# Two-block transformer on one core: in the attention of layers 0 and 1, TensorE multiplies by the values and turns the values ahead of the next step's scores instead of behind them

## The chip, the cores and the metric

One core of a Trainium2 chip runs the whole program. The metric is the device time of one launch in microseconds (us), the median over several runs.

## What is computed

Two blocks of two transformer layers each, in float32, on 512 latent tokens and 256 context tokens of width 1024. Layers 0 and 1 (the first block) hold the attention that the change touches: four heads, and in each head two softmax maps over the same keys, of which the second is subtracted with a weight:

```
def diff_attn(q, k, v, lam):
    s = jnp.einsum("bqhmd,bkhmd->bhmqk", q.astype(F32), k.astype(F32)) * (B_QK_DIM ** -0.5)
    p = jax.nn.softmax(s, axis=-1)
    a = p[:, :, 0] - lam * p[:, :, 1]
    return jnp.einsum("bhqk,bkhd->bqhd", a, v.astype(F32))
```

The latent queries attend to all 768 tokens. In layer 0 the 256 context queries attend to the 256 context tokens as well; in layer 1 the context has no queries. Around the attention stand the input projection, a gated part, a convolution, the output projection and a feed-forward part, and the second block has other kinds of attention; none of that changes.

## The kernel before

Every engine has its own list of instructions, written out in Python and executed in order; the engines meet through semaphores. Weights pass through a ring of slots, are split into a high and a low part, and TensorE forms each linear layer as three products. Nearly every matmul is issued by the helper `mm`, line 1161, so that line names scores, products with values and linear layers alike; they are told apart by their operands.

**Steps and rounds.** `Attention.__init__` (from line 721) cuts the attention into steps: for each head four blocks of 128 latent queries, and in layer 0 a fifth step with both blocks of context queries (keys: 256). That makes 20 steps in layer 0 and 16 in layer 1. TensorE's `attention` (the loop `for n in range(A.n)` from line 1645) runs in rounds. Round n holds, for step n-3, the turns of the finished map (`turn`, line 1552: six 128x128 transposes through PSUM, in two groups of three, p0 and p1; for a context step one group of four), then the scores of step n+1 (`scores`), and behind them what else the planner put in this round (`rr[2:]`): either the product of the turned maps with the values (`values`, operands `PTR` and `VT`) of the pair of blocks that ends at step n-4, or the turns of a later head's values (line 1558, a group of four, v0, and one of two, v1). Products come in every second latent round. In a round whose map is a context step there is only one group of map turns, so the product is the second entry and already stands ahead of the scores.

Where the planner's list `rr` is made (lines 766 to 788), each entry gets a number r, counted through the layer. Turns and products all write the bank `AUX`:

```
        def turn_bank(r):

            return AUX[:, 512 * (r["n"] % 2):512 * (r["n"] % 2) + 512]
```

Its two halves alternate by number, and `bank_free` makes entry r wait until entry r-2 has been read out.

**The other engines.** VectorE's `attention` finds the maxima of step n+1 for both maps (line 2875, the `TENSOR_REDUCE`), inverts the sums of the exponentials and subtracts the maps (line 2912). GpSimd scales the first map (line 1056). ScalarE's `attention` runs, in round n, in this order: the exponentials of step n's first map (`exps(n, 0)`, line 2143), the copy of the product of round n-1 out of the bank (line 2129), the copies of this round's map turns into `PTR` (line 2118), the exponentials of the second map, and at the end the copies of turned values (line 2122).

**Score buffers.** The scores of the two maps take three PSUM buffers in turn, `PS[(2 * n + e) % 3]`, so `scores(n + 1)` waits for `exps(n, 0)` before it overwrites the buffer.

`keep_clock` in round 2 issues seven idle-time matmuls; it keeps its place.

Of the kernel before, what the change touches and what calls it, by code (L numbers as in the profile page):

```python
# [109 lines left out]
def build(nc, d, out):  # L110
# [81 lines left out]
    with ctx:  # L192
# [266 lines left out]
        for li, L in enumerate(layers):  # L459
# [18 lines left out]
            for part, rr in enumerate((rows, second)):  # L478
                r, todo = 0, []
# [58 lines left out]
        def stat_use(li, name):  # L538

            return len(STAT_USES) * li + STAT_USES.index(name)  # L540
# [613 lines left out]
        def _(pe):  # L1154
# [15 lines left out]
            def keep_clock(n, bank):  # L1170

                for _ in range(n):
                    mm(bank[:, 0:P], IDENT, IDENT, True, True)

            def tile(t, kc, toks, hi, lo, out=None, mid=None, chunk=None, spare=False, ctx_ready=None):

                slot = t % 2
                pe.wait_ge(S.hi_ready, t + 1)
                if t >= 2 and not spare:
                    pe.wait_ge(S.tile_free, t if out is not None else t - 1)  # L1180
                out = AUX if spare else LIN[slot] if out is None else out
                for a, n in spans(toks):
                    if a and ctx_ready:
                        ctx_ready()
                    for k in range(kc):
                        if chunk and a == 0:
                            chunk(k)
                        mm(out[:, a:a + n], whi(t)[:, k, :], hi[:, k, a:a + n], k == 0, False)
                        mm(out[:, a:a + n], whi(t)[:, k, :], lo[:, k, a:a + n], False, False)
                if mid:  # L1190
                    mid()
                pe.wait_ge(S.lo_ready, t + 1)
                for a, n in spans(toks):
                    for k in range(kc):
                        last = mm(out[:, a:a + n], wlo(t)[:, k, :], hi[:, k, a:a + n], False, k == kc - 1)
                last.then_inc(S.tile_done, 1)
# [57 lines left out]
            def piece(t, i):  # L1254

                if i == 0:
                    pe.wait_ge(S.hi_ready, t + 1)
                if i == 2:
                    pe.wait_ge(S.lo_ready, t + 1)
                for a, n, high, ks in (((0, LAT, True, range(0, 5)),), ((0, LAT, True, range(5, 8)), (LAT, CTX, True, range(0, 4))),  # L1260
                                       ((LAT, CTX, True, range(4, 8)), (LAT, CTX, False, range(8))), ((0, LAT, False, range(8)),))[i]:
                    for k in ks:
                        if high:
                            mm(AUX[:, a:a + n], whi(t)[:, k, :], HH[:, k, a:a + n], k == 0, False)
                            mm(AUX[:, a:a + n], whi(t)[:, k, :], HL[:, k, a:a + n], False, False)
                        else:
                            last = mm(AUX[:, a:a + n], wlo(t)[:, k, :], HH[:, k, a:a + n], False, k == DC - 1)
                if i == 3:
                    last.then_inc(S.tile_done, 1)
# [254 lines left out]
            def attention(A, L):  # L1524
# [105 lines left out]
                def step(r):  # L1630

                    (values if r["kind"] == "o" else turn)(r)
# [12 lines left out]
                for n in range(A.n):  # L1645
                    rr = A.rounds[n]
                    if n == 0 and A.diff:
                        pe.wait_ge(S.stat_read, stat_use(li, "turn V0") + 1)
                    for i in A.pieces.get(n, ()):
                        piece(A.late.t0, i)  # L1650
                    if n and n - 1 == A.evac_at:
                        pe.wait_ge(S.tile_free, A.late.t0 + 1)
                    for r in rr[:2]:
                        step(r)
                    if n in A.tiles:
                        x = A.tiles[n]
                        hi, lo = (CQH, CQL) if x.kc == 6 else (CKH, CKL)
                        tile(x.t0, x.kc, x.toks[0], hi, lo, STAT)
                    if A.mla:
                        for r in rr[2:]:  # L1660
                            step(r)
                    if n < 3:
                        keep_clock(((13, 0, 0) if A.mla else (0, 0, 7) if A.diff else (0, 8, 0))[n], STAT if A.mla else AUX)
                    if n + 1 < len(A.steps):
                        for part in range(2):
                            scores(n + 1, part)
                    if not A.mla:
                        for r in rr[2:]:
                            step(r)
                pe.wait_ge(S.exp_done, A.sides_end())  # L1670
# [19 lines left out]
            for li, L in enumerate(layers):  # L1690
# [86 lines left out]
                if blk == 0:  # L1777
                    pe.wait_ge(S.norm_used, norm_at(li, "Q3") + 1)
                    pe.wait_ge(S.mod_copied, 1)
                    pe.wait_ge(S.half_read, half_use(li, "w_s") + 1)  # L1780
                    attention(L["attention"], L)
                    rs_read()
                    head_sums, head_spread = norm_parts(T, False, big)
# [9 lines left out]
                elif l == 0:  # L1793
                    pe.wait_ge(S.qk_ready, w.seen(S.qk_ready))
                    pe.wait_ge(S.swap_landed, 32)
                    attention(L["attention"], L)
                else:
                    key_sums, key_spread = norm_parts(TOK, False, lambda c: RCK[:, c, :])
                    query_sums, query_spread = norm_parts(LAT, False, lambda c: RCQ[:, c, :])
                    n0 = w.made.get(S.rs_done, 0)  # L1800
                    def latent_jobs(j):
                        if j == 3:
                            rs_read()
                            key_sums(n0, (0, 1))
                        if j == 4:
                            key_spread(n0)
                    linear(L["w_in"], HH, HL, None, S.h_ready, mid=latent_jobs, pause=9)
                    q0, k0, v0 = L["heads"][0]
                    pe.wait_ge(S.cq_ready, w.seen(S.cq_ready, 2))
                    linear(k0, CKH, CKL)  # L1810
                    query_sums(n0 + 1, range(6))
                    linear(v0, CKH, CKL)
                    query_spread(n0 + 1)
                    keep_clock(14, AUX)
                    w.seen(S.mix_hi, 4 * 2 + 2)
                    linear(L["q_rope"], CQH, CQL, None, S.cq_ready, range(6))
                    linear(q0, CQH, CQL)
                    rs_read()
                    attention(L["attention"], L)
# [1643 lines left out]
```

## Time and profile before

| | us |
|---|---|
| median of 3 runs | 3516.88 |
| lowest and highest of them | 3513.91, 3517.04 |
| the profiled execution's own time | 3513.67 |
| its span | 3511.8 |
| TensorE busy in the span | 3347.6 (95%) |
| VectorE busy | 2041.3 (58%) |
| ScalarE busy | 1311.6 (37%) |
| GpSimd busy | 432.6 (12%) |
| mean granted TensorE clock | 0.992 |

The profile comes from one execution, whose own time lies 2 us above its span. Times in it count from the start of the span. The attention of layer 0 stands at about 263 to 366 us, that of layer 1 at about 1177 to 1262 us. In a timeline row the first number is the start, the second the time until the group's last instruction ended; consecutive TensorE groups overlap a little, since the ends of matmuls are modelled. A float32 matmul stands there as two instructions, a transpose as one, so a product of six matmuls reads x12. The bracket at a row's end is the idle time of the engine ahead of it and what ended that.

### The profile page before, as it was taken

Reading aid. Unit: us, or ns where it says so; the run is one execution under the profiler, and the core shown is the slowest. Engines: PE = TensorE matmul, PEld = TensorE weight load, DVE = VectorE, ACT = ScalarE, POOL = GpSimd, SP = SyncE. Lnnn points to the kernel's source line nnn. Section 1 sums busy time; section 2 is a strip of 40 time slices with the busy share of each in tenths; the row PEclk is TensorE's granted clock in tenths of the full one; section 3 lists DMA queues with packets and bytes.
Section 4 is the critical chain, followed back from the end, with each engine's and each line's share of the span. In section 5 each row is a group of like instructions: output and inputs, shape, how many; then the busy total and the mean of one; then the engine's idle time right before and its main releaser. Section 6 shows DMA issues by size and latency. Waiting matters only on the chain.

```text
span 3511.8 us, 47116 instructions
## 1 busy us (share of the span) xinstructions
PE 3347.6 (95%) x18692; PEld 2722.9 (78%) x18692; DVE 2041.3 (58%) x3251; ACT 1311.6 (37%) x2000; POOL 432.6 (12%) x387
## 2 busy tenths in 40 slices
PE   7998999999999999999998889999999999999998
PEld 5775888888887677888886577888888866668886
DVE  4757467545568647878435746654556455565345
ACT  3436342112234544223334544321223545444233
POOL 2005530000000320000003521000001023200000
PEclk9999999999999999999999999999999999999999
DMA  6440233333322113546221212442432311123332
GB/s 213 130 127 13 59 76 124 126 98 131 118 67 67 31 49 120 191 161 204 69 59 25 43 32 62 131 134 88 132 124 57 68 29 31 33 70 103 95 101 74
DMA packets 477242, 321.86 MB, mean 92 GB/s; under 512 B 54872, under 2 KB 450558, under 8 KB 477024
## 3 DMA queue, kind: packets, MB, share of 16 engines
q1 hardware_dynamic: 467104, 304.13, 28.6%
q0 software_dynamic: 9920, 14.71, 1.7%
q8 instruction: 150, 2.46, 0.3%
q14 instruction: 68, 0.56, 0.0%
HBM read 313.20 MB, written 3.57 MB: 90 GB/s over the span
## 4 chain that ended last, share of the span: by engine, by line
PE 81%; DVE 9%; ACT 5%; issue 3%; DMA 1%; POOL 1%; DVEq 0%; SPq 0%; ACTq 0%; POOLq 0%
PE PS L1161 78%; PE PS L1552 3%; DVE CPROD L3053 2%; DVE TMP L2743 1%; ACT BIG L2143 1%; DVE TMP L3371 1%; ACT TMP L2064 1%; DVE HL L2751 1%; DVE ATT L2875 1%; ACT SPH L1881 1%; ACT HH L2067 0%; DVE CACC L3151 0%; DMA XSTG<-in_x 0%; DMA RAW<-in_w_in 0%; DVE SPL L2558 0%
## 5 line engine op out<-in xcount | busy, mean ns | idle before, releaser
L1161 PE MATMUL PS<-HH,SPH 128*128 128x512 f32 (+1 forms) x3336 | 1138.3, 354 | 29.7 <-ACT HH L2067 11.3
L1161 PE MATMUL PS<-HL,SPH 128*128 128x512 f32 (+1 forms) x3336 | 1112.3, 352 | 3.8 <-DVE HL L2751 1.3
L1161 PEld LDWEIGHTS PS<-HH,SPH 128*128 128x128 f32 x3336 | 632.3, 190 | 142.2 <-issue 33.2
L1161 PE MATMUL PS<-HH,SPL 128*128 128x512 f32 (+1 forms) x3336 | 705.9, 354 | 0.0
L1161 PEld LDWEIGHTS PS<-HL,SPH 128*128 128x128 f32 x3336 | 628.6, 190 | 93.1 <-DVE HL L2751 8.5
L2558 DVE TENSOR_TENSOR SPL<-RAW,SPH 128x1024 fp32r<-128x1024 f32 (+3 forms) x358 | 447.1, 1249 | 333.3 <-ACT SPH L1881 333.2
L1161 PEld LDWEIGHTS PS<-HH,SPL 128*128 128x128 f32 x3336 | 560.9, 190 | 93.7 <-issue 7.6
L1881 ACT ACTIVATE SPH<-RAW 128x1024 fp32r<-128x1024 f32 (+3 forms) x358 | 383.7, 1072 | 522.3 <-PE PS L1161 449.5
L1161 PE MATMUL PS<-MH,SPH 128*128 128x512 f32 (+1 forms) x1067 | 362.5, 354 | 0.8 <-ACT SPH L1881 0.8
L1161 PE MATMUL PS<-ML,SPH 128*128 128x512 f32 (+1 forms) x1067 | 359.8, 352 | 0.0
L3371 DVE SCALAR_TENSOR_TENSOR TMP<-PS,PCOL,TMP 128x511 f32<-128x511 f32 (+1 forms) x264 | 174.3, 660 | 222.8 <-ACT TMP L2493 210.1
L2988 DVE SCALAR_TENSOR_TENSOR X<-PS,MOD,X 128x512 f32<-128x512 f32 (+1 forms) x139 | 92.0, 662 | 355.9 <-PE PS L1161 354.1
L3053 DVE CUSTOM_DVE_ANT_0 CPROD<-MS,CB 128x1024 f32<-128x1024 f32 x224 | 274.5, 1226 | 29.5 <-DVE SM L3374 10.4
L1161 PEld LDWEIGHTS PS<-MH,SPH 128*128 128x128 f32 x1067 | 201.8, 189 | 29.6 <-ACT SPH L1881 1.6
L1161 PEld LDWEIGHTS PS<-ML,SPH 128*128 128x128 f32 x1067 | 201.9, 189 | 27.5 <-issue 0.2
L2875 DVE TENSOR_REDUCE ATT<-PS 128x1 f32<-128x768 f32 x160 | 146.1, 952 | 121.2 <-PE PS L1161 121.1
L1161 PE MATMUL PS<-MH,SPL 128*128 128x512 f32 (+1 forms) x1067 | 213.5, 353 | 0.0
L1161 PEld LDWEIGHTS PS<-MH,SPL 128*128 128x128 f32 x1067 | 177.4, 189 | 27.8
L2493 ACT ACTIVATE TMP<-PS,PCOL 128x768 f32<-128x768 f32 (+1 forms) x88 | 78.0, 886 | 312.1 <-PE PS L1161 311.8
L1056 POOL TENSOR_SCALAR BIG<-BIG,ATT 128x768 f32<-128x768 f32 (+2 forms) x61 | 129.1, 2122 | 454.4 <-DVE ATT L2885 454.4
L2502 ACT ACTIVATE MH<-TMP 128x768 fp32r<-128x768 f32 (+1 forms) x88 | 65.1, 739 | 264.2 <-DVE TMP L3378 264.2
L1056 POOL TENSOR_SCALAR TMP<-TMP,ATT 128x768 f32<-128x768 f32 (+2 forms) x56 | 116.7, 2088 | 242.3 <-DVE ATT L2885 242.3
(360 smaller groups left out, 3639.9 us busy)
## 6 DMA issues: line engine op xcount, KB each, us to landing
MS<-in_mod_turned SPq DMA_DIRECT2D x144, 512.0 KB, 5.3
RAW<-in_l_w_up SPq DMA_DIRECT2D x88, 512.0 KB, 4.0
RAW<-in_w_gate SPq DMA_DIRECT2D x44, 512.0 KB, 4.2
RAW<-in_w_val SPq DMA_DIRECT2D x44, 512.0 KB, 4.2
RAW<-in_w_down SPq DMA_DIRECT2D x32, 704.0 KB, 4.7
RAW<-in_l_w_down SPq DMA_DIRECT2D x32, 704.0 KB, 4.6
RAW<-in_w_in SPq DMA_DIRECT2D x40, 512.0 KB, 4.6
MS<-in_w_mod SPq DMA_DIRECT2D x32, 512.0 KB, 4.7
```

Source lines behind the costliest of these rows:

```text
L1056: last = pool.tensor_scalar(ex, ex, inverse_col(n, e, b), None, ALU.mult)
L1161: return pe.matmul(o, a, b, start=start, stop=stop)
L1552: last = pe.transpose(bank[:, k * P:(k + 1) * P], A.slot(m, e)[:, at:at + P], IDENT)
L1881: act.activation(whi(t)[:, 0:kc, :], RAW[slot][:, 0:kc, :], ACT.Copy).then_inc(S.hi_ready, 1)
L2064: act.activation(TMP[c % 2][:, a:a + m], X[:, c, a:a + m], ACT.Identity, scale=MUL[:, k, n, c:c + 1], bias=MODS[li % 2][:, n, 24 * k + c:2 ...
L2493: act.activation(TMP[0][:, 0:T], up_place(up, j, s)[:, 0:T], ACT.Identity, scale=par(li, "fw", FFC + fc), bias=par(li, "fb", fc))\
L2502: act.activation(MH[:, f, 0:T], TMP[1][:, 0:T], ACT.Copy)\
L2558: dve.tensor_tensor(wlo(t)[:, 0:kc, :], RAW[slot][:, 0:kc, :], whi(t)[:, 0:kc, :].bitcast(F32), ALU.subtract).then_inc(S.lo_ready, 1)
L2875: dve.tensor_reduce(top_col(n, e), A.scores(n, e), AX.XY if A.mla else AX.X, ALU.max, negate=True)\
L2988: dve.scalar_tensor_tensor(out=xc, in0=up_place(x, j, s)[:, a:a + k], scalar=g, in1=xc, op0=ALU.mult, op1=ALU.add)\
L3053: dve.tensor_tensor_reduce(out=CPROD[:], in0=MS[m % 2][:].rearrange("p k c -> p (k c)"), in1=CB[:, v, :], scale=1.0, scalar=0.0, op0=ALU.m ...
L3371: dve.scalar_tensor_tensor(out=g[:, a + da:a + da + m - 1], in0=ps[:, a + sa:a + sa + m - 1], scalar=tap(k), in1=g[:, a + da:a + da + m - ...
```

## The change

Two conditions on TensorE's loop. In layers 0 and 1 (`A.diff`) all entries of a round's list are executed ahead of the scores; before, two of them were, and the rest came behind. The second block's layers keep their order.

```
                    if n and n - 1 == A.evac_at:
                        pe.wait_ge(S.tile_free, A.late.t0 + 1)
-                    for r in rr[:2]:
+                    for r in rr if A.diff else rr[:2]:
                         step(r)
...
                     if n + 1 < len(A.steps):
                         for part in range(2):
                             scores(n + 1, part)
-                    if not A.mla:
+                    if not A.mla and not A.diff:
                         for r in rr[2:]:
                             step(r)
```

The numbering of the entries, the bank waits and the lists of the other engines stay as they were: VectorE, ScalarE, GpSimd and the DMA queue have the same instructions in the same order. On TensorE these entries move across one set of scores: in layer 0 three products of latent pairs (rounds 5, 10, 15), three products of context steps (rounds 8, 13, 18) and three sets of value turns (rounds 4, 6, 9); in layer 1 five products (rounds 5, 7, 9, 11, 13) and three sets of value turns (rounds 4, 6, 8). Behind the last scores nothing changes.

TensorE in layer 1, rounds 11 and 12 and the map turns of round 13 (`CST,BIG` or `CST,TMP` are map turns, `BIG` alone scores, `PTR,VT` the product). Before:

```order
L1552 MATMUL PS<-CST,BIG 128x128 x6
L1161 MATMUL PS<-BIG 128x512 x2
L1161 MATMUL PS<-BIG 128x256 x2
L1161 MATMUL PS<-PTR,VT 128x256 x6
L1552 MATMUL PS<-CST,BIG 128x128 x6
L1161 MATMUL PS<-BIG 128x512 x2
L1161 MATMUL PS<-BIG 128x256 x2
L1552 MATMUL PS<-CST,TMP_67 128x128 x6
```

and with the change:

```order
L1552 MATMUL PS<-CST,BIG 128x128 x6
L1161 MATMUL PS<-PTR,VT 128x256 x6
L1161 MATMUL PS<-BIG 128x512 x2
L1161 MATMUL PS<-BIG 128x256 x2
L1552 MATMUL PS<-CST,BIG 128x128 x6
L1161 MATMUL PS<-BIG 128x512 x2
L1161 MATMUL PS<-BIG 128x256 x2
L1552 MATMUL PS<-CST,TMP_67 128x128 x6
```

The product with values of round 11 stood behind the scores of step 12 and now stands ahead of them, right behind the map turns of its own round. The four rows behind it are the same.

TensorE in layer 0 from round 8, whose product belongs to a context step (x2), over round 9 with value turns (L1558), to the product of round 10. Before:

```order
L1552 MATMUL PS<-CST,BIG 128x128 x6
L1161 MATMUL PS<-BIG 128x256 x4
L1161 MATMUL PS<-PTR,VT 128x256 x2
L1552 MATMUL PS<-CST,TMP_67 128x128 x6
L1161 MATMUL PS<-BIG 128x512 x2
L1161 MATMUL PS<-BIG 128x256 x2
L1558 MATMUL PS<-CST,BIG 128x128 x6
L1552 MATMUL PS<-CST,BIG 128x128 x6
L1161 MATMUL PS<-BIG 128x512 x2
L1161 MATMUL PS<-BIG 128x256 x2
L1161 MATMUL PS<-PTR,VT 128x256 x6
```

and with the change:

```order
L1552 MATMUL PS<-CST,BIG 128x128 x6
L1161 MATMUL PS<-PTR,VT 128x256 x2
L1161 MATMUL PS<-BIG 128x256 x4
L1552 MATMUL PS<-CST,TMP_67 128x128 x6
L1558 MATMUL PS<-CST,BIG 128x128 x6
L1161 MATMUL PS<-BIG 128x512 x2
L1161 MATMUL PS<-BIG 128x256 x2
L1552 MATMUL PS<-CST,BIG 128x128 x6
L1161 MATMUL PS<-PTR,VT 128x256 x6
L1161 MATMUL PS<-BIG 128x512 x2
```

Three entries moved, each ahead of the scores of its round: the short product of the context step, the six value turns and the product of six matmuls; the scores themselves keep their succession.

## Rows read from the trace of the kernel before

**Rows 1.** The page, chain of work that ended last, by engine:

```profile
PE 81%; DVE 9%; ACT 5%; issue 3%; DMA 1%; POOL 1%; DVEq 0%; SPq 0%; ACTq 0%; POOLq 0%
```

**Rows 2.** Windows: from:to length, busy PE, PEld, DVE, ACT, POOL, granted clock, DMA share, GB/s:

```profile
282.35:302.31 19.96, 15.88 (x90) 11.01 (x90) 17.64 (x32) 16.13 (x39) 14.23 (x6) 1.00 0.05 14
302.31:351.94 49.63, 40.44 (x214) 26.20 (x213) 34.83 (x66) 31.21 (x78) 29.95 (x14) 0.97 0.00 0
1192.15:1244.36 52.21, 45.44 (x233) 29.75 (x233) 38.68 (x73) 35.72 (x81) 37.04 (x12) 0.93 0.02 6
```

**Rows 3.** Timeline of PE, layer 1: start, length, engine, line, operation [idle before]:

```profile
1226.20 1.56 PE L1161 MATMUL PS<-BIG 64*128 64x512 f32 x8
1227.69 0.88 PE L1552 MATMUL PS<-CST,BIG 128*128 128x128 f32 x6
1229.98 1.56 PE L1161 MATMUL PS<-BIG 64*128 64x512 f32 x8 [1.41 <-ACT BIG L2143]
1231.47 2.86 PE L1161 MATMUL PS<-PTR,VT 128*128 128x256 f32 x12
...
1235.28 1.56 PE L1161 MATMUL PS<-BIG 64*128 64x512 f32 x8
...
1244.36 1.56 PE L1161 MATMUL PS<-BIG 64*128 64x512 f32 x8
...
1248.43 2.86 PE L1161 MATMUL PS<-PTR,VT 128*128 128x256 f32 x12 [1.70 <-ACT PTR L2118]
```

**Rows 4.** Timeline of ACT and DVE, layer 1, rounds 11 and 12:

```profile
1225.28 0.38 ACT L2129 ACTIVATE BIG<-PS 128x256 f32<-128x256 f32 x1 [0.78 <-PE PS L1161]
...
1225.61 0.49 ACT L2118 ACTIVATE PTR<-PS 128x384 f32<-128x384 f32 x1
...
1226.31 0.49 ACT L2118 ACTIVATE PTR<-PS 128x384 f32<-128x384 f32 x1 [0.20 <-PE PS L1552]
...
1227.79 1.82 DVE L2875 TENSOR_REDUCE ATT<-PS 128x1 f32<-128x768 f32 x2 [2.06 <-PE PS L1161]
1228.84 0.90 ACT L2143 ACTIVATE BIG<-PS,ATT 128x768 f32<-128x768 f32 x1 [1.16 <-DVE ATT L2875]
...
1229.73 0.86 ACT L2118 ACTIVATE PTR<-PS 128x384 f32<-128x384 f32 x2
```

**Rows 5.** Timeline of PE, layer 0, rounds 11 to 13 (a product ahead of scores):

```profile
319.91 1.56 PE L1161 MATMUL PS<-BIG 64*128 64x512 f32 x8
...
321.89 2.76 PE L1161 MATMUL PS<-PTR,VT 128*128 128x256 f32 x12
324.58 1.56 PE L1161 MATMUL PS<-BIG 64*128 64x512 f32 x8
...
328.55 0.55 PE L1552 MATMUL PS<-CST,TMP 128*128 128x128 f32 x3 [1.93 <-ACT BIG L2129]
```

**Rows 6.** Timeline of PE and ACT, layer 0, around the context steps:

```profile
285.96 0.87 ACT L2118 ACTIVATE PTR<-PS 128x384 f32<-128x384 f32 x2
...
306.75 1.14 PE L1161 MATMUL PS<-BIG 64*128 64x256 f32 x8
307.82 1.13 PE L1161 MATMUL PS<-PTR,VT 128*128 128x256 f32 x4
308.78 0.49 PE L1552 MATMUL PS<-CST,TMP 128*128 128x128 f32 x3
...
309.62 0.38 ACT L2129 ACTIVATE BIG<-PS 128x256 f32<-128x256 f32 x1
```

**Rows 7.** Windows of single intervals between two sets of scores (columns as in 2):

```profile
329.02:333.75 4.73, 4.65 (x20) 3.02 (x19) 3.05 (x9) 3.27 (x9) 3.65 (x2) 0.64 0.00 0
1192.15:1196.49 4.34, 3.66 (x14) 2.09 (x15) 3.86 (x8) 3.15 (x8) 3.61 (x2) 0.59 0.20 60
1196.49:1202.13 5.64, 4.79 (x20) 2.73 (x21) 4.32 (x8) 3.92 (x10) 4.07 (x2) 0.71 0.00 0
1207.43:1211.52 4.09, 3.25 (x22) 2.00 (x21) 2.60 (x5) 3.27 (x8) 2.31 (x2) 1.00 0.00 2
```

**Rows 8.** Timeline of PE: first and last of the six longest gaps:

```profile
282.35 1.13 PE L1161 MATMUL PS<-BIG 64*128 64x256 f32 x8 [1.94 <-ACT BIG L2143]
...
1192.15 2.19 PE L1161 MATMUL PS<-BIG 64*128 64x512 f32 x8 [1.94 <-ACT BIG L2143]
```

More of the change, by code:

```diff
@@ L1652, in attention @@
                         pe.wait_ge(S.tile_free, A.late.t0 + 1)
-                    for r in rr[:2]:
+                    for r in rr if A.diff else rr[:2]:
                         step(r)
@@ L1666, in attention @@
                             scores(n + 1, part)
-                    if not A.mla:
+                    if not A.mla and not A.diff:
                         for r in rr[2:]:
```

## The prediction

> **What bounds the kernel now.** I read the page's chain first: 81% of it is TensorE [rows 1]. But the engine's share over the span says little about the two stretches that the change touches, so I cut windows there. From the scores of step 4 to those of the last step, TensorE is busy 15.88 + 40.44 = 56.3 of 69.6 us in layer 0 and 45.44 of 52.21 us in layer 1, and no other engine is busier [rows 2]. TensorE has gaps, so something else carries the rhythm. The timeline shows what. Take the scores of step 11 as zero, 1226.20 [rows 3]. VectorE starts the first maximum at 1.59, ScalarE the first exponentials at 2.64; they end and ScalarE goes on to its copies at 3.53 [rows 4]; the next scores start at 3.78, after a TensorE gap of 1.41 that ends on these exponentials [rows 3]. This is a loop: scores, maximum, exponentials, scores. Nothing in it but the scores is TensorE's, and a round can't be shorter than 3.78 us.
>
> The next interval, 1229.98 to 1235.28, takes 5.30 us: behind the scores stands a product that TensorE issues for 2.7 us (321.89 to 324.58, [rows 5]), while the maximum and exponentials of the loop run beside it. About 2.2 us of each product are thus under the loop's own waits; what sticks out is 5.30 - 3.78 = 1.52 us. **The reader should see that the gap stands ahead of the scores, and that its end (first exponentials) also starts ScalarE's copies.** The question is whether a product can use that gap.
>
> **What a moved product has to wait for.** Its half of the bank was last written by p0, the first map turns of its own round. ScalarE copies p0 only behind the first exponentials of the round, in the old order and in the new. So the product ahead of the scores cannot start in the gap: it starts at the gap's end and later. The trace of before has this very case. Behind the last scores of layer 1 (1244.36) there are no more scores to go ahead, and the product of round 15 follows its map turns directly: it starts at 1248.43, having waited 1.70 us for the `PTR` copy [rows 3]. That is 4.07 us after the scores. With the product's 2.69 the next scores start at **6.76** instead of 3.78. Nobody else could have been late: the scores are queued behind the product, VectorE's maximum behind the scores, ScalarE's exponentials behind the maximum.
>
> The round after it gets something back, since no product stands behind its scores. It doesn't fall to 3.78: the second group of map turns, p1, waits until the product is copied out, and that copy again stands behind the first exponentials. Layer 0 shows this order too, since in rounds 7, 12 and 17 the product is already ahead: after 324.58, p1 starts at 328.55, having waited 1.93 us for the copy [rows 5], and the next scores at 329.02 [rows 7], so **4.44**. In those rounds the product itself doesn't wait, since only one group of map turns precedes it and its bank was read in the round before; the interval is 324.58 - 319.91 = 4.67. Even that pair, 4.67 + 4.44 = 9.11, is no better than the 3.78 + 5.30 = 9.08 of the old order. The moved products give 6.76 + 4.44 = 11.20, **2.1 us more a pair**.
>
> **Short products and value turns.** A context product (four instructions) takes 308.78 - 307.82 = 0.96 us [rows 6]. Moved ahead, it waits for p1 (ends at 4.44) and for the copy of p0 (product copy at 3.53, p0's copy 0.33 behind it, 0.49 long: 4.35, [rows 4]), so the next scores start at 4.45 + 0.96 = **5.41** instead of 4.44; I take nothing off in the following round, where p1 waits for the exponentials either way. Value turns v0 wait for the copy of p0 and v1 for that of p1. With a product to copy first, p1's copy starts 1.03 behind it [rows 4], at 4.56, and ends at 5.05; 0.05 to start (a copy of p0 that began at 3.53 and took 0.49 let the product go at 4.07) and 0.36 for two turns (three and the way to the scores take 0.47) make **5.46**. Without a product: 3.53 + 0.86 + 0.05 + 0.36 = **4.80**; in round 4 of layer 0, whose step is a context step, the copies start at 285.96, 3.61 after scores at 282.35 [rows 6, 8], hence 4.89; in round 9 the product's copy starts at 309.62, 2.87 after its scores [rows 6], hence 2.87 + 1.03 + 0.49 + 0.41 = 4.80.
>
> **The sum**, interval by interval against the windows [rows 2]:
> - Layer 0, rounds 4 to 7: 4.89 + 6.76 + 5.46 + 4.68 = 21.79 against 19.96: +1.8.
> - Layer 0, rounds 8 to 18: three short products 16.23, value turns 4.80, two long products 13.52, two rounds behind a long one 8.88, two unchanged rounds 12 and 17 9.36, round 14 at its old 4.73: 57.52 against 49.63: +7.9.
> - Layer 1, rounds 4 to 14: value turns 4.80, five products 33.80, two rounds with value turns behind a product 10.92, three plain ones behind a product 13.32, and 2.1 of low clock that stands in before and that I leave (next part): 64.95 against 52.21: +12.7.
>
> Together **+22.5 us**. Behind the last scores nothing moves. Neither layer's end has slack that could take it up: the output projection starts from what the attention leaves, and TensorE carries the chain there. Map maxima, subtractions and GpSimd's scaling get more time per round than before and cost nothing; GpSimd is busy 37 of 52 us in the tightest stretch [rows 2]. No DMA is moved, and each engine but TensorE has the same list.
>
> **The clock.** Three intervals of before show a granted clock of 0.59 to 0.71, that is partly at 1.2 instead of 2.4 GHz, and cost 4.73 - 3.78 = 0.95, 4.34 - 3.78 = 0.56 and 5.64 - 4.09 = 1.55 us; the last is measured against an interval with the same entries at full clock [rows 7]. These are two falls, at 1.5 us on average. Each came directly behind a gap of about 1.93 us on TensorE; there are six such gaps (the first ends at 282.35, the last at 1192.15, [rows 8]), so one in three was followed by a fall. The new order makes eight more of them, p1 waiting for a product's copy (rounds 6, 11, 16 and 6, 8, 10, 12, 14), and eight of 1.70 like the one at 1248.43, behind which the product ran at full speed [rows 3]. Bounds: no fall at all, the old ones gone too, -3 us; a fall behind each of the sixteen, +24 us. I take eight thirds of 1.5, **+4 us**, as nearest to the rows.
> The Trainium skill (TensorE: Matmul & The Clock Gate, Part 4) says that PE-mode transposes do not count as busy for the clock in the same way and don't get the full clock. By this rule the gaps would be longer than they look, as only transposes stand at their sides, and the high bound would be nearer. The trace speaks against its strong form: six transposes took 0.88 us at full granted clock between 1226 and 1230, where nothing slowed [rows 3].
>
> So 3513.67 + 22.5 + 4 = 3540.2 for the profiled execution; the median of the runs shown lies 3.2 above it, which gives **3543 us**, 0.75% more. A measurement of this kernel tells about 0.2%, 7 us, from no change.
>
> **Rivals.**
> *The clock decides (12%).* A fall behind most new gaps: 3539.5 + 12 to 24, say 3558 us. For it: one in three of the old gaps, and the new rounds come without pause between. Against it: three gaps between 282 and 291 in a row at 1.00 [rows 2]. It decides from about eight falls on.
> *The gap is filled (5%), no slower than before.* If the product started right behind p1, at about 2.3 us after the scores, the pair would be 5.1 (scores 1.5, turns 0.8, product 2.7) + 3.78 = 8.9 instead of 9.08, a gain of 0.2 us over some ten pairs, and the value turns would vanish in the gap: 3514 us. The point is whether the bank is free at 2.3 or at 4.07 us. For it only a bank wait that isn't where I read it; against it the waiting product at 1248.43 [rows 3] and the 4.44 us behind a product ahead [rows 5, 7].
> The Trainium skill (Perfetto Trace Analysis, Optimization Strategies) sets as a general goal to keep the matmul engine as busy as possible. Work placed into its gap would follow that and give this rival's time; the same sentence goes on to those engines that block the critical path, and here that is ScalarE.
>
> **How the numbers follow.** The forecast has 83%. Its own range is 3543 less 7 (no falls) and less some 4 for other runs, up to 12 more for twice the falls and for errors of 0.3 us in some twenty intervals. Taken to the clock rival's middle: 3531 to 3558. Slower by over 0.2%: 94%, the forecast, the clock rival and a little less for what I misread; the filled gap gives same 4% and faster 2%.
>
> **What would show it.** In layer 1, between plain scores: intervals alternating 6.8 and 4.4 us where 3.8 and 5.3 stood; the moved product with about 1.7 us idle before it, ended by the `PTR` copy; p1 with 1.9 us idle, ended by line 2129; the window of layer 1 that was 52.2 at about 65 us, that of layer 0 that was 69.6 at about 79; everything outside the two attentions as before. Wrong would be: products that start 2.3 us after their scores, or a granted clock under 0.85 over either attention, or a difference outside of them.

## The result

The changed kernel takes 3559.95 us (median of 4 runs, 3550.11 to 3561.84) against 3516.96 us before; the ratio is 1.0120, with a 95% interval from 1.0108 to 1.0132. It is slower by 43 us. The forecast was slower by 26.5 us, 3543 us, in a range up to 3558, so the time lies 2 us above the range (one of the four runs, 3550.11 us, lies inside it). One run of the kernel before in this comparison took more than twice its usual time and is left out of the ratio.

The profiled execution took 3561.84 us with a span of 3560.0 us, 48.2 more than before. The page's chain by engine hardly differs from [rows 1]:

```profile
PE 81%; DVE 9%; ACT 5%; issue 3%; DMA 1%; POOL 0%; DVEq 0%; SPq 0%; ACTq 0%; POOLq 0%
```

So the place must be looked for in the windows. The same stretches as [rows 2], from the scores of step 4 to those of the last step (layer 0, then layer 1; in the columns of rows 2):

```profile
286.24:373.92 87.68, 67.02 (x306) 42.49 (x306) 53.04 (x100) 47.37 (x119) 45.10 (x19) 0.86 0.01 4
1217.15:1289.21 72.06, 52.76 (x233) 33.14 (x233) 38.20 (x71) 34.84 (x81) 36.12 (x12) 0.86 0.02 5
```

Layer 0 had 69.6 us there and has 87.7, layer 1 had 52.2 and has 72.1: together 37.9 of the 48.2 us. The granted clock of both stretches is 0.86, where it was 0.97 to 1.00 and 0.93. Of the other 10.3 us, 4.1 lie in the rounds behind the last scores: 17.99 us to the first matmul behind the attention in layer 0, where 15.35 stood, and 19.57 against 18.09 in layer 1. There, too, a product became slow, 5.49 us in layer 0 where 2.86 stood:

```profile
377.22 0.94 PE L1552 MATMUL PS<-CST,BIG 128*128 128x128 f32 x6 [1.69 <-ACT BIG L2129]
...
379.64 5.49 PE L1161 MATMUL PS<-PTR,VT 128*128 128x256 f32 x12 [0.74 <-ACT PTR L2118]
```

The last 6.2 us lie outside both attentions, 3.9 of them before the scores of step 4 in layer 0. Up to there TensorE has the same list in all the kernels below that have no fills, and in their traces these scores start anywhere between 281.9 and 286.5 us, so this much is scatter between executions. Behind the second attention the two filled kernels below, with the same list there, differ by 3.0 us.

TensorE's timeline of layer 1, from the p1 turns of round 10 to the scores of step 14, answers to [rows 3] and [rows 5]:

```profile
1262.82 0.89 PE L1552 MATMUL PS<-CST,BIG 128*128 128x128 f32 x3 [1.92 <-ACT BIG L2129]
1263.64 2.85 PE L1161 MATMUL PS<-BIG 64*128 64x512 f32 x8
1266.42 0.88 PE L1552 MATMUL PS<-CST,BIG 128*128 128x128 f32 x6
1269.00 4.54 PE L1161 MATMUL PS<-PTR,VT 128*128 128x256 f32 x12 [1.70 <-ACT PTR L2118]
1273.47 1.56 PE L1161 MATMUL PS<-BIG 64*128 64x512 f32 x8
1274.97 0.55 PE L1552 MATMUL PS<-CST,BIG 128*128 128x128 f32 x3
1277.44 0.55 PE L1552 MATMUL PS<-CST,BIG 128*128 128x128 f32 x3 [1.92 <-ACT BIG L2129]
1277.91 1.56 PE L1161 MATMUL PS<-BIG 64*128 64x512 f32 x8
1279.40 0.88 PE L1552 MATMUL PS<-CST,TMP 128*128 128x128 f32 x6
1281.98 2.86 PE L1161 MATMUL PS<-PTR,VT 128*128 128x256 f32 x12 [1.70 <-ACT PTR L2118]
1284.77 1.56 PE L1161 MATMUL PS<-BIG 64*128 64x512 f32 x8
```

Two pairs of rounds stand in it. In the second, everything is at full clock: the product starts 4.07 us after its scores (1281.98 - 1277.91), the next scores at 6.86, and the interval behind them is 4.44. In the first the order and the waits are the same, but scores take 2.85 instead of 1.56 and the product 4.54 instead of 2.86, and the interval is 9.83. Windows show why: three in a row through the first pair, cut where the granted clock changes, and one over the second pair's product interval:

```profile
1262.86:1266.27 3.41, 3.41 (x11) 1.63 (x11) 0.82 (x3) 1.66 (x4) 2.60 (x1) 0.50 0.00 0
1266.27:1269.69 3.42, 1.72 (x11) 1.28 (x10) 3.10 (x6) 2.11 (x5) 1.18 (x1) 1.00 0.00 0
1269.69:1273.10 3.41, 3.41 (x10) 2.70 (x9) 0.10 (x1) 0.52 (x2) 1.85 (x1) 0.50 0.00 0
1277.91:1284.77 6.86, 5.16 (x28) 3.53 (x27) 3.58 (x9) 4.00 (x9) 5.20 (x2) 1.00 0.00 0
```

The granted clock falls to half (1.2 GHz) as p1 starts behind the gap of 1.92 us, stays there through p1 and the scores, and is back at full by 1266.27, just before the map turns start. It stays full through these turns and the gap of 1.70 us, and falls again 0.7 us after the product has started.

Read in the same way, the clock fell eleven times in the two stretches and once more behind the last scores of each layer, thirteen times in all, each time within 1.6 us of the end of a gap. Five falls came in moved products of six matmuls, which took 4.54 us; the other three moved products took 2.86 us. Two came behind p1's new gaps of 1.92 us, of which there are eight. Three came behind a gap that the forecast did not list: behind a moved context product, too, the next turns wait for its copy, 1.7 us where 0.8 stood (the turns that start at 320.02, 350.85 and 377.22):

```profile
320.02 0.55 PE L1552 MATMUL PS<-CST,TMP 128*128 128x128 f32 x3 [1.69 <-ACT BIG L2129]
320.40 1.43 PE L1558 MATMUL PS<-CST,BIG 128*128 128x128 f32 x6
321.76 2.75 PE L1161 MATMUL PS<-BIG 64*128 64x512 f32 x8
```

The last three stand behind gaps of 1.9 us that the kernel before has as well; behind two of them it has its own two falls.

And the waits of TensorE (in total, times, longest), layer 0 and then layer 1:

```profile
PE PS L1552 <- ACT BIG L2129: 16.6, 9, 1.9
PE PS L1161 <- ACT PTR L2118: 5.4, 4, 1.7
...
PE PS L1161 <- ACT PTR L2118: 10.2, 7, 1.7
PE PS L1552 <- ACT BIG L2129: 9.6, 5, 1.9
```

The waits are the forecast ones: map turns for the product's copy (line 2129), products for the map turns' copy (line 2118). The open question was whether the waits cost what was worked out, and whether the clock makes up all of the rest.

### The profile page after: what moved, and what is told of

Read it like the earlier page. It is cut to its first block, busy times and chain, and to the rows that moved or that the text cites. A ratio compares the mean times of both kernels' runs of the same rounds, so it can differ in the third digit from the quotient of the medians.

```text
span 3560.0 us, 47116 instructions
## 1 busy us (share of the span) xinstructions
PE 3374.5 (95%) x18692; PEld 2738.9 (77%) x18692; DVE 2041.8 (57%) x3251; ACT 1309.2 (37%) x2000; POOL 432.3 (12%) x387
## 4 chain that ended last, share of the span: by engine, by line
PE 81%; DVE 9%; ACT 5%; issue 3%; DMA 1%; POOL 0%; SPq 0%; DVEq 0%; ACTq 0%; POOLq 0%
PE PS L1161 77%; PE PS L1552 3%; DVE CPROD L3053 2%; DVE ATT L2875 1%; ACT BIG L2143 1%; DVE TMP L2743 1%; DVE TMP L3371 1%; ACT TMP L2064 1%; DVE HL L2751 1%; ACT PTR L2118 1%; ACT SPH L1881 0%; DMA RAW<-in_w_in 0%; DVE CACC L3151 0%; ACT HH L2067 0%; ACT TMP L2143 0%
```

## The experiments

Times are medians; the kernel before took 3515.46 to 3516.05 us beside them.

### Fill the gaps of the changed kernel, and those of the kernel before

Idle-time matmuls go ahead of the first map turns of a round, into the bank half that these turns overwrite. The waits stay.

```
+                def fill(r, count):
+                    if count:
+                        bank_free(r)
+                        keep_clock(count, turn_bank(r))
...
+                    if A.diff and 3 <= n < len(A.steps) - 1:
+                        if any(q["kind"] == "o" for q in A.rounds[n - 1]):
+                            fill(rr[0], 5 if A.steps[n][0]["nj"] == 2 else 7)
+                        else:
+                            fill(rr[0], 7 if n == 3 else 3 if n == 4 else 5 if rr[2:] and rr[2]["kind"] == "o" else 0)
                     for r in rr if A.diff else rr[:2]:
                         step(r)
```

> The changed kernel, with idle-time matmuls (of the kind that keep_clock issues) ahead of the first map turns of a round, 3 to 7 of them as the gap is long, in the rounds whose scores follow. They write the half of the bank that the map turns then overwrite. Theory (waits and clock): the changed kernel lost 22.5 us to waits behind ScalarE and about 20 us to low clock in the products that follow the gaps; with the gaps filled TensorE stays at full clock in both attentions, the products take 2.86 us instead of 4.54, and the time is 3536 to 3543 us. Rival (the 20 us are no matter of the clock, or the waits are longer than worked out): it stays at 3555 to 3565 us, or goes up, since more work stands ahead of the turns.

Measured: 3540.58 us, ratio 1.0077 (1.0062 to 1.0092), 19 us less than the changed kernel, although TensorE has more to do. The theory's time; the rival is out. The windows of its two stretches:

```profile
283.06:361.71 78.65, 72.47 (x446) 52.32 (x446) 53.04 (x100) 47.37 (x119) 45.09 (x19) 1.00 0.02 5
1207.51:1270.95 63.44, 57.92 (x358) 41.97 (x358) 38.19 (x71) 34.84 (x81) 36.10 (x12) 1.00 0.02 5
```

The clock is 1.00, and the stretches are 9.0 and 8.6 us shorter than in the changed kernel. Behind the last scores there are no fills, and there layer 0 still has a slow product (4.96 us). Each interval stands at the full-clock value: 6.86 with a product, 4.44 behind it, 5.45 with value turns, 5.40 with a context product. The product is no longer slow:

```profile
1249.85 1.38 PE L1161 MATMUL PS<-CST 128*128 128x128 f32 x10
1251.07 0.82 PE L1552 MATMUL PS<-CST,BIG 128*128 128x128 f32 x6
1252.43 2.86 PE L1161 MATMUL PS<-PTR,VT 128*128 128x256 f32 x12 [0.54 <-ACT PTR L2129]
1255.22 1.56 PE L1161 MATMUL PS<-BIG 64*128 64x512 f32 x8
```

(Line 2129 is here the copy of map turns; the added lines shift the numbers.)

The same for the kernel before, in its own gaps:

```
+                    if A.diff and 3 <= n < len(A.steps) - 1 and not A.rounds[n - 1][2:]:
+                        if any(q["kind"] == "o" for q in A.rounds[n - 1]):
+                            fill(rr[0], 7)
+                        elif not any(q["kind"] == "o" for q in rr[:2]):
+                            fill(rr[0], 7 if n < 5 else 5)
                     for r in rr[:2]:
                         step(r)
```

> The kernel before, with the same kind of idle-time matmuls in its own gaps (5 or 7 ahead of the map turns, in rounds without a product behind the last scores). Theory: its two falls of the clock cost 3 us, so 3512 to 3516 us, and no interval in the attentions below a granted clock of 1.00. Rival (fills cost as much as they give back, as the map turns come later): 3517 to 3522 us.

Measured: 3513.56 us, ratio 0.9998 (0.9988 to 1.0007). Its windows are at full clock:

```profile
285.44:354.07 68.63, 62.27 (x368) 43.85 (x368) 52.47 (x98) 47.06 (x117) 44.14 (x19) 1.00 0.02 4
1196.12:1246.33 50.21, 46.45 (x266) 32.23 (x266) 38.57 (x73) 35.78 (x81) 37.01 (x12) 1.00 0.02 6
```

The two falls of [rows 7] are gone, and the stretches are 1.0 and 2.0 us shorter. Two microseconds in the whole time can't be told from none by the interval; the windows tell them. With these two kernels the order alone is priced at full clock: 78.65 - 68.63 = 10.0 us in layer 0 and 63.44 - 50.21 = 13.2 us in layer 1, together **23.2 us**. (The medians of the two lie 27.0 us apart. The slow product behind the last scores of layer 0 takes 2.4 of the rest, and what is left is within the scatter outside the attentions.)

### Move only a part

```
-                    for r in rr[:2]:
+                    early = [r for i, r in enumerate(rr) if i < 2 or A.diff and r["kind"] == "o" and A.steps[r["step"]][0]["nj"] > 2]
+                    for r in early:
                         step(r)
...
                         for r in rr[2:]:
-                            step(r)
+                            if r not in early:
+                                step(r)
```

> The kernel before, with only the products of six matmuls moved ahead of the scores (3 in layer 0, 5 in layer 1); value turns and context products stay behind them. Theory: each costs 6.8 + 4.4 against 3.8 + 5.3 us, 2.1 us, together 17 us at full clock, and since a product follows a gap it also pays for most of the falls, 12 to 18 us: 3544 to 3552 us. Rival (the 43 us are spread evenly over the 17 moved entries, 2.5 us each): 3537 us.

Measured: 3545.69 us, ratio 1.0091 (1.0074 to 1.0108). The other kernel has the condition turned round (`not (...)`):

> The complement: only the three context products and the six sets of value turns moved ahead, the products of six matmuls stay behind the scores. Theory: 1 us for each context product and 0.7 to 1.1 us for each set of value turns, 8 us, and few falls since the gaps stay short: 3523 to 3530 us. Rival (spread evenly, 9 entries at 2.5 us): 3540 us.

Measured: 3526.39 us, ratio 1.0031 (1.0019 to 1.0043). Both lie where the theory put them and well away from an even spread. The parts add up: 30.2 + 10.9 = 41.1 us against 43. The eight long products carry three quarters of it. Low clock is in both: within the two stretches the first trace has eleven falls, and the second six, where few were expected.

### Take the waits away

ScalarE's order within a round, in layers 0 and 1, on top of the change:

```
                     if n < len(A.steps):
                         exps(n, 0)
                     if not A.mla:
-                        if n:
+                        if n and not outs_first:
                             read_outs(n - 1)
-                        for r in early:
-                            read_turn(r)
+                        if not turns_first:
+                            for r in early:
+                                read_turn(r)
```

with `read_outs(n - 1)` and the copies of the map turns ahead of `exps(n, 0)` where the two new conditions hold. First only the product's copy goes ahead (`outs_first = A.diff and n`, `turns_first` false):

> The changed kernel, and on ScalarE in layers 0 and 1 the copy of the finished product (of the round before) goes ahead of the first exponentials instead of behind them. Theory (waits behind the first exponentials): the second group of map turns no longer waits, intervals behind a product shrink from 4.44 to 3.8 us and those with value turns from 5.45 to 4.8, some 13 times 0.65 us = 8 us; products still start 4.1 us after their scores. Low clock somewhat less often, since gaps of 1.9 us become 1.4. 3540 to 3552 us. Rival (the map turns wait for something else): 3557 to 3562 us as the changed kernel.

Measured: 3537.64 us, ratio 1.0062 (1.0048 to 1.0076), a little below what was expected. The intervals behind a product shrank to 3.78 us. In layer 0, one interval behind a context step became 3.12 us, where the filled kernel has 3.78; it ends on the exponentials. Products still start some 4.1 us after their scores, and four of eight are still slow.

Then both copies go ahead (`turns_first = A.diff`):

> The changed kernel, and on ScalarE in layers 0 and 1 both the copy of the finished product and the copies of this round's map turns go ahead of the first exponentials. Theory: the bank is then free at 2.4 us, the product starts there instead of at 4.1 and fills the gap, product intervals 5.2 instead of 6.86 us, the others 3.8 to 4.1 (exponentials late by the copies in front of them), falls of the clock as rare as in the kernel before: 3514 to 3524 us. Rival (a product ahead of the scores costs its full length wherever it starts): 3545 us or more.

Measured: 3513.87 us, ratio 0.9993 (0.9984 to 1.0002): **46 us less than the changed kernel, with TensorE's order untouched.** That is the whole loss, clock included: its two stretches have no fall. The rival, that a product ahead of the scores costs its length wherever it starts, is out. The intervals are 5.40 and 3.97.

Last, the map turns' copies go ahead only in rounds whose product or value turns stand ahead of scores (`turns_first = A.diff and A.rounds[n][2:] and n < len(A.steps) - 1`):

> As the run before it, but the map turns' copies go ahead of the exponentials only in rounds with a product or value turns ahead of the scores; in the others the exponentials go first again. Theory: 0.3 us less in each plain interval than with the copies always first, 5.2 + 3.8 = 9.0 us a pair against 9.08 in the kernel before: 3510 to 3518 us, no faster than the kernel before by anything that can be measured. Rival: as for the run before.

Measured: 3509.77 us, ratio 0.9987 (0.9978 to 0.9996). This is just below the expected range, and against the expectation the interval tells it from the kernel before. TensorE and ScalarE in layer 1, rounds 12 and 13:

```profile
1231.92 1.56 PE L1161 MATMUL PS<-BIG 64*128 64x512 f32 x8 [1.41 <-ACT BIG L2143]
...
1233.41 0.88 PE L1552 MATMUL PS<-CST,TMP 128*128 128x128 f32 x6
...
1234.00 0.87 ACT L2118 ACTIVATE PTR<-PS 128x384 f32<-128x384 f32 x2 [0.58 <-PE PS L1552]
1234.54 2.86 PE L1161 MATMUL PS<-PTR,VT 128*128 128x256 f32 x12 [0.25 <-ACT PTR L2118]
1234.75 0.90 ACT L2143 ACTIVATE BIG<-PS,ATT 128x768 f32<-128x768 f32 x1
...
1237.33 1.56 PE L1161 MATMUL PS<-BIG 64*128 64x512 f32 x8
```

The copies now run while ScalarE would wait for a maximum, and the product starts 2.62 us after the scores, with 0.25 us idle before it. The interval is 5.41, that behind it 3.78. A pair is 9.19 us, which is no better than the 9.08 of before; the windows show where the gain lies:

```profile
281.88:347.08 65.20, 55.57 (x306) 37.03 (x307) 53.08 (x98) 46.56 (x119) 41.97 (x19) 1.00 0.02 5
1190.51:1241.11 50.60, 42.67 (x233) 28.02 (x233) 37.54 (x71) 34.73 (x81) 35.46 (x12) 1.00 0.02 7
```

Layer 1 needs 0.4 us more than the filled kernel before, layer 0 needs 3.4 less. There the map turns around context steps waited for product copies in the order of before too (4.44 and 3.77 us, now 3.97 and 3.09), which makes 2.1 us; the other 1.3 lie in rounds 4 to 7, where value turns moved ahead of the scores.

### Cut the product in two

```
+                    cut_now = [r for r in rr[2:] if A.diff and r["kind"] == "o" and A.steps[r["step"]][0]["nj"] > 2 and n + 1 < len(A.steps)]
                     for r in rr[:2]:
                         step(r)
+                    for r in cut_now:
+                        values(r, 0)
...
-                            step(r)
+                            if r in cut_now:
+                                values(r, 1)
+                            else:
+                                step(r)
```

`values(r, 0)` issues the first three of the six matmuls and `values(r, 1)` the rest, with the scores in the middle of the accumulation. ScalarE's map-turn copies go first in rounds with a product behind the scores, its product copies in the round behind such a round.

> The order of before (value turns and context products behind the scores), but a product of six matmuls is cut in two: three ahead of the scores, three behind, in one accumulation. In its round ScalarE copies the map turns ahead of the first exponentials, and in the round behind it the product. Theory: three matmuls (1.35 us) fill the gap that the loop leaves in one interval, three stand under the loop of the other: about 3.9 + 4.3 instead of 3.8 + 5.3 us, 0.9 us less for each of eight products, and fewer falls: 3503 to 3511 us, faster than both kernels. Rival (the first half delays the scores by its whole length, and nothing is saved behind): 3515 to 3525 us.

Measured: 3517.36 us, ratio 1.0006 (0.9998 to 1.0015). This is a miss: the rival's time. The cut products of this kernel don't hold the right sums (why is open), so it stands for the times of the order alone. The order did what it should in the plain rounds: 4.11 and 4.50 us, 8.61 a pair instead of 9.08. But it was lost again where value turns stood behind the scores and before a round with a cut product: those intervals grew to 5.46, where the kernel before has 4.1, because the half product ahead of the scores waits for map turns that wait for the value turns' copies. A fall of the clock stayed, too, in one interval of 7.16 us in layer 1. Here the forecast looked at one pair of rounds and not at its neighbours.

### Which gaps let the clock fall

The first fill, in two parts: only in rounds 3 and 4 and behind a product (the gap of 1.9 us, p1 waiting), and only in rounds 3 and 4 and ahead of a product (the gap of 1.7 us). In the code the other `fill` becomes `pass` or 0.

> The changed kernel with idle-time matmuls in rounds 3 and 4 and ahead of the map turns of every round behind a product, where p1 waits 1.9 us; the gaps of 1.7 us ahead of the products of six matmuls stay open. It tells which gaps let the clock fall. Theory now (the trace of the changed kernel shows five of eight moved products that took 4.5 us instead of 2.9 right behind a gap of 1.7 us): these gaps carry half or more of the 19 us, 3547 to 3554 us. Rival (as forecast: only the 1.9 us gaps matter, the 1.7 us gaps do nothing): 3540 to 3543 us, as with all gaps filled.

Measured: 3540.93 us, ratio 1.0071 (1.0057 to 1.0085), as with all gaps filled. The theory fell and the rival, which was the assumption of the forecast, stands in this respect. The trace makes it less simple, though. Two of the eight products were still slow:

```profile
1240.57 4.54 PE L1161 MATMUL PS<-PTR,VT 128*128 128x256 f32 x12 [1.70 <-ACT PTR L2129]
...
1253.55 2.86 PE L1161 MATMUL PS<-PTR,VT 128*128 128x256 f32 x12 [1.70 <-ACT PTR L2129]
```

Of these two products one is slow and one is not, and both stand behind the same gap of 1.70 us, so the length of the gap alone doesn't decide.

> The complement: idle-time matmuls in rounds 3 and 4 and in the 1.7 us gaps ahead of the products of six matmuls, the 1.9 us gaps of the map turns behind a product stay open. Theory now: products at full clock, scores behind some of the turn gaps at low clock: 3543 to 3549 us. Rival (only the 1.9 us gaps matter): 3554 to 3558 us.

Measured: 3547.49 us, ratio 1.0091 (1.0075 to 1.0106), in the theory's range. With the products' gaps filled, it is the scores behind the open 1.9 us gap that are slow:

```profile
1260.07 0.55 PE L1552 MATMUL PS<-CST,BIG 128*128 128x128 f32 x3 [1.92 <-ACT BIG L2140]
1260.55 2.93 PE L1161 MATMUL PS<-BIG 64*128 64x512 f32 x8
...
1265.99 2.86 PE L1161 MATMUL PS<-PTR,VT 128*128 128x256 f32 x12 [0.28 <-ACT PTR L2129]
```

By the medians, filling the turn gaps gives back all of the 19 us and filling the product gaps 12. The profiled executions say how much of that lies in the two stretches, first with the turn gaps filled, then with the product gaps:

```profile
283.45:362.10 78.65, 68.99 (x416) 48.84 (x417) 53.03 (x100) 47.38 (x119) 45.09 (x19) 1.00 0.02 4
1205.26:1272.07 66.81, 55.51 (x309) 38.52 (x309) 38.20 (x71) 34.85 (x81) 36.12 (x12) 0.95 0.02 4
287.64:375.23 87.59, 69.81 (x342) 45.50 (x343) 53.03 (x100) 47.51 (x119) 45.14 (x19) 0.88 0.01 3
1218.36:1285.83 67.47, 54.55 (x288) 36.82 (x288) 38.19 (x71) 35.00 (x81) 36.13 (x12) 0.92 0.02 4
```

Against the changed kernel's 87.68 and 72.06 us these are 14.3 and 4.7 us less; all fills together gave 17.6. So the turn gaps carry the greater part, and the product gaps gave nothing in layer 0. Yet in the changed kernel only two falls came behind p1's new gaps and five came in products. With the turn gaps filled, two products were slow instead of five, although the gaps ahead of them stayed as they were. So a fall depends on more than the gap right ahead of it. What else counts is not shown: each row is one execution, and a fill changes the idle time and the kind of matmul at once.

### A version that beats both

The kernel with ScalarE's selective order, measured again in more rounds, and with fills in the gaps that it leaves:

> The same kernel as in the run called e7_after_sel (the change, with ScalarE's copies of products first, and those of map turns first in rounds with a product or value turns), measured again in more rounds. Theory: 3508 to 3514 us, 0.1 to 0.2% faster than the kernel before. Rival (the difference was chance): 3515 to 3518 us.

Measured: 3510.97 us, ratio 0.9988 (0.9980 to 0.9997). It repeats.

> As the run before it, with idle-time matmuls in the gaps that it leaves: 7 in round 3 and 5 in each round without product and value turns (gap 1.4 us). Theory: no interval of the two attentions at low clock, 2 us less than without them: 3506 to 3512 us. Rival: no difference, 3508 to 3514 us.

```
+                    if A.diff and 3 <= n < len(A.steps) - 1 and (n < 4 or not rr[2:] and not any(r["kind"] == "o" for r in rr)):
+                        fill(rr[0], 7 if n == 3 else 5)
```

Measured: 3507.69 us, ratio 0.9982 (0.9973 to 0.9990). It is faster than the kernel before by 0.2% and than the changed one by 52 us. Its lead over the unfilled one, 3 us, is within what the intervals leave open, and the traces don't show it: the two stretches take 65.23 and 50.59 us here and 65.20 and 50.60 in the first trace without fills, all at a clock of 1.00.

## Why the prediction was wrong, point by point

**What bounds the stretches: right.** The loop of scores, maximum, exponentials and scores carries the rhythm; a change of ScalarE's order alone took the whole loss away.

**What a moved product waits for: right.** 4.07 us from scores to product was forecast and measured. The interval was forecast at 6.76 and is 6.86: the product's 2.69 us left out some 0.1 us that passes between a product that had to wait and the scores behind it (1284.77 - 1281.98 = 2.79). Behind a product 4.44 was forecast and measured, with value turns behind a product 5.46 against 5.45, with a context product 5.41 against 5.40. Value turns without a product behind them took 4.79 to 4.95 us against 4.80 to 4.89. One slip has no effect: of a product of 2.7 us that sticks out by 1.52, not "about 2.2" but 1.2 us are hidden.

**The sum of the waits: right.** 22.5 us were forecast, 23.2 us measured at full clock. "Behind the last scores nothing moves" held for the waits; the 4.1 us that were lost there are low clock.

**The clock: wrong, and this is the step that failed.** The prediction took "eight thirds of 1.5", +4 us: one fall behind every third of eight new gaps of 1.9 us, none behind the 1.7 us gaps. In the profiled execution low clock costs the changed kernel 9.0 + 8.6 us in the two stretches and 4.1 behind the last scores, 21.7 together; the kernel before has 3.0 of it. The term is thus **18.7 us where 4 were forecast**, and the waits with it make 41.9 of the 48.2 us; the rest is the scatter outside. What a fall costs was nearly right: 1.5 us against 21.7 / 13 = 1.7. The number was off: thirteen falls, where two old and eight thirds of new ones were counted. Of the sixteen new gaps named, seven had a fall, and mostly not those expected: five in products behind 1.7 us gaps, where none was allowed for, and two behind the eight gaps of 1.9 us. Three came behind the 1.7 us gaps after moved context products, where the prediction took no new wait into account for the clock, and one behind an old gap that had none before. The rate had been taken from six gaps of a kernel in which a round with a gap has one with a long product beside it, and from one single product behind a 1.7 us gap. The changed kernel puts a gap in nearly every round, and these ratios don't carry over. The upper bound of 24 us was the better guide. Why the clock falls at one gap and not at its like stays open.

**Transposes and the clock.** The trace of the changed kernel has six transposes in 0.88 us at a granted clock of 1.00 (1266.42) and in 1.54 us at half clock (1291.16), so they do run at full clock where it is granted. The prediction had weighed this and left its high bound alone. The Trainium skill (TensorE: Matmul & The Clock Gate, Part 4) speaks of transposes as not counting for the clock in the same way, which would make each of the new gaps longer by the turns beside it, and most of all p1's gaps of 1.92 us, with turns on both sides. The fills speak for that, since filling these gaps gave back most; against it, only two of these eight gaps had a fall behind them, and five of the eight ahead of products, with turns on one side. So the runs don't decide on the rule.

**The rivals.** The clock rival, priced at 12%, named 3558 us and a decision "from about eight falls on"; there were thirteen, and the time was 3560. Its condition, a fall behind most of the new gaps, held for seven of the sixteen that it knew. It deserved far more, and the range should have reached up to its sum, 3563. The filled gap didn't occur, because the bank was free at 4.07 us, as argued; once the copies went first, the gap was filled and the time was 3513.87 us, against 3514 in the rival's sum. That match is partly luck: the pair takes 5.40 + 3.97 = 9.37 us, not 8.9, and layer 0's context rounds make up for it.

**The signs named beforehand.** Gaps of 1.7 and 1.9 us and their releasers came as named. Of intervals alternating between 6.8 and 4.4 us only those at full clock did. A granted clock under 0.85 was named as a sign of error; it was 0.86 over both stretches, just short of it. The windows were forecast at 65 and 79 us and are 72 and 88. A difference outside the attentions was named as well, and 6 of the 48 us in the profiled executions lie there; the traces of kernels that are the same up to the first attention differ by as much.

## What to carry to other kernels

Moving work into an engine's idle time only helps if the work can start when the idle time does: follow its buffer back to the instruction that frees it. Here that instruction stood behind the very event that ended the gap, and two lines of order on the other engine (copies ahead of exponentials) turned 43 us of loss into a gain of a few. And where a change turns overlapped work into alternating bursts and gaps on TensorE, price the clock as its own term, with one fall a new gap as its bound, and count every gap that the change makes; a few idle-time matmuls in the gaps tell by experiment what it is.

## What was not expected of the hardware

TensorE's clock went to half and back twice within some ten microseconds: 0.50, 1.00 and 0.50 in the three windows from 1262.86 to 1273.10. Neither change sits where one would look for it. It was back at full just before the slow scores ended, it stayed full through six transposes and 1.70 us of idle time, and it fell when TensorE had been at work on the product again for 0.7 us. Equal gaps of 1.70 us had a slow product behind them in five cases and a fast one in two. In the changed kernel the low clock is worth 19 us of 3560, nearly as much as the waits themselves.
